# Low halves of weight groups moved three projection pieces behind the high halves, and the W products moved in front of the search's update

## The chip, the cores and the metric

The kernel runs on one core of one Trainium2 chip. The metric is device time in microseconds (us) for one execution, the median of several runs.

## The reference, cut to what matters

One decoder layer over 1024 tokens of width 1024. One input projection feeds three head groups: a gated DeltaNet (4 heads of 128, short causal convolution on q, k and v, chunked delta rule), a sparse attention whose keys are picked by a small indexer (top 256 of up to 1024 keys a token), and a cross-attention into 256 memory tokens.

```python
h = x @ w_in[l]                                   # all projections of the layer
qkv = silu(_short_conv(concat([q_a, k_a, v_a]), conv_w[l]))
# DeltaNet, per head and chunk:
sol = triangular_solve(m, concat([v * beta, k_beta * exp(g)]))   # u, w
def step(state, inp):
    v_new = u_i - w_i @ state
    o = qg @ state + a_i @ v_new
    state = state * gl + kd.T @ v_new
# sparse attention, per token:
score = sum_j(relu(q_idx_j @ k_idx) * w_idx_j)    # then the 256 largest
_, idx = lax.top_k(score, topk)
...
y = concatenate([o_a, o_s, o_m]) @ w_out[l]
x = _layernorm(DEEPNORM_ALPHA * x + y, ln_g[l], ln_b[l])
```

## The kernel before

`make_plan` writes one list of steps; every engine walks it in order and executes what belongs to it, waiting on semaphores. So the place of a step in the list sets its place in the queue of each engine that has part in it. `woven` mixes three things: the steps of the DeltaNet solve and scan of one head, the projection work of the next head (`todo`), and the search for the 256th largest score. A bare number in `steps` is a stretch; in it the plan places a due `update`, then projection units, then one `count` group.

**Projections.** The weights come in 32 groups of 128 columns; 30 of them are split. Products are made in three matmuls of 512 columns: high by high, high by low, low by high (L862 to L864). A *piece* is two of eight chunks of one half of the tokens, that is 6 matmuls; a group has 8 pieces. A group is split by `("split", name)`: ScalarE copies the raw weights to the high half (in the trace `ring_split<-ring`, L1598), VectorE subtracts to get the low half (L1254, `ring_split<-ring,ring_split`, both inputs in SBUF). `with_splits` puts the split of a group where the group before it begins. TensorE waits for the low half before a group's first piece.

**Search.** 32 rounds find the threshold bit by bit. In each, ScalarE counts with six activations (`count`, L1681, widths 1024, 384, 896, 512, 768, 640), and VectorE makes the next candidate in six small operations (`update`, L1307 to L1324) that wait for the six counts; the first count of the next round waits for L1323.

**Solve and scan of head h.** Block inverses are refined by levels (`M`, `XY`). Then `GB` and `KB` prepare the keys of head h+1: VectorE scales the two halves of the keys (L1422 and L1423, each twice; their other input is in PSUM), GpSimd multiplies SBUF by SBUF (L1856 and L1861, each twice, 128x512). `nw` makes the W products of head h (L1043 on TensorE, two copies L1598 `arena<-bank` on ScalarE), needed from the second scan step. `scanV` b (L1051, L1057; copy to `vnew` by VectorE, L1458) and `scanS` b (L1068, L1072, L1073; new state `dn_s` by VectorE, L1466 or L1468; output added by VectorE, L1227 or L1230) alternate over b = 0 to 7. The values' convolution taps (L1216 to L1220) stand between them. Four PSUM banks of pool "D" go round, so the output product of step 0 takes the bank that the first `nw` copy frees.

The order of `("nw", h)` stands in these lines of the plan:

```python
                steps += [*keys_scaled(after)[0], 1.5, *keys_scaled(after)[1], 1.5]
            else:
                steps += [1.5, 1.5]
...
        steps += [*pair("nw", h), 1]
```

## Time and profile before

| | before |
|---|---|
| median of 3 runs | 856.08 us (855.95 to 856.45) |
| profiled execution, device time | 857.43 us |
| its span | 855.6 us |
| mean granted TensorE clock | 0.961 |
| TensorE busy | 764.7 us (89%) |
| VectorE busy | 492.4 us (58%) |
| ScalarE busy | 461.6 us (54%) |
| GpSimd busy | 145.9 us (17%) |

The span is from the first to the last instruction; the device time lies 1.83 us above it. Busy shares are averages over stages: start and index scores to about 160 us, the four DeltaNet heads to about 576 us, attention and output after that. A row of the trace gives the start, the duration, the engine and the line, and in brackets how long the engine had been idle before it and what ended the idle time.

### The profile page before, as it was taken

How to read it: one execution, taken by the hardware profiler on the slowest of the kernel's cores; microseconds unless marked ns; L12 is line 12 of the kernel's file. 1: busy time of each engine (PE TensorE's matmuls, PEld its weight loads, DVE VectorE, ACT ScalarE, POOL GpSimd, SP SyncE). 2: the span in 40 equal slices, each digit the busy share in tenths (PEclk: the TensorE clock that was granted, in tenths of full speed). 3: DMA queues.
4: the chain of work that ended last, by engine and by line, in shares of the span. 5: the costliest groups of instructions: out<-in, count | busy, mean ns of one | idle time of the engine just before them, and what ended most of it. 6: DMA issues, size and time to landing. Idle time of an engine off the chain costs nothing.

```text
span 855.6 us, 11422 instructions
## 1 busy us (share of the span) xinstructions
PE 764.7 (89%) x3996; PEld 621.1 (73%) x3996; DVE 492.4 (58%) x1068; ACT 461.6 (54%) x1045; POOL 145.9 (17%) x248
## 2 busy tenths in 40 slices
PE   6999969899997899789998899885798998998975
PEld 5888858688886789678886788663466776774764
DVE  5633868846655475554654477853556456636532
ACT  5423566789768875888768742224543333332310
POOL 0000000063011510142111420001003033302330
PEclk9999979999999999999998999997889999999998
DMA  9312110125002320023001231009201122121201
GB/s 358 101 50 75 49 38 26 37 66 140 27 26 65 86 82 25 26 77 105 25 26 62 59 124 50 25 33 311 99 1 62 39 72 87 55 60 46 74 25 49
DMA packets 56424, 60.87 MB, mean 71 GB/s; under 512 B 16048, under 2 KB 42928, under 8 KB 55984
## 3 DMA queue, kind: packets, MB, share of 16 engines
q1 hardware_dynamic: 56368, 60.15, 21.4%
q8 instruction: 32, 0.52, 0.2%
q14 instruction: 24, 0.20, 0.1%
HBM read 45.46 MB, written 14.68 MB: 70 GB/s over the span
## 4 chain that ended last, share of the span: by engine, by line
PE 62%; DVE 16%; ACT 13%; issue 6%; DMA 2%; SPq 1%; POOL 0%; DVEq 0%; ACTq 0%; POOLq 0%
PE bank L854 16%; PE bank L862 9%; PE bank L864 9%; PE bank L863 9%; PE bank L868 3%; ACT cst L1681 3%; PE bank L1098 2%; PE bank L1126 2%; PE bank L1018 2%; PE bank L1033 2%; PE bank L1031 2%; PE bank L1005 1%; DVE score L1301 1%; ACT ring_split L1598 1%; DVE mix_lo L1548 1%
## 5 line engine op out<-in xcount | busy, mean ns | idle before, releaser
L862 PE MATMUL bank<-x_hi,ring_split 128*128 128x512 f32 x480 | 200.4, 417 | 7.6 <-DVE x_lo L1246 7.2
L864 PE MATMUL bank<-x_hi,ring_split 128*128 128x512 f32 x480 | 190.9, 398 | 0.0
L863 PE MATMUL bank<-x_lo,ring_split 128*128 128x512 f32 x480 | 190.7, 397 | 0.0
L1681 ACT ACTIVATE cst<-score,sel 128x1024 bf16<-128x1024 f32 (+2 forms) x192 | 166.9, 874 | 24.7 <-DVE sel L1323 24.7
L862 PEld LDWEIGHTS bank<-x_hi,ring_split 128*128 128x128 f32 x480 | 92.6, 193 | 23.4 <-DVE ring_split L1254 7.9
L864 PEld LDWEIGHTS bank<-x_hi,ring_split 128*128 128x128 f32 x480 | 92.1, 192 | 20.6
L863 PEld LDWEIGHTS bank<-x_lo,ring_split 128*128 128x128 f32 x480 | 92.7, 193 | 15.3
L1598 ACT ACTIVATE arena<-bank 128x512 f32<-128x512 f32 (+1 forms) x108 | 49.7, 499 | 35.0 <-PE bank L868 10.5
L1782 ACT ACTIVATE arena<-arena,misc 128x512 f32<-128x512 f32 (+7 forms) x32 | 24.8, 775 | 80.5 <-DVE misc L1518 80.5
L1254 DVE TENSOR_TENSOR ring_split<-ring,ring_split 128x1024 fp32r<-128x1024 f32 x30 | 38.8, 1295 | 43.0 <-ACT ring_split L1598 42.9
L854 PE MATMUL bank<-w_out_hi,mix_hi 128*128 128x512 f32 x128 | 56.0, 437 | 6.7 <-DVE mix_lo L1548 4.2
L1568 DVE SCALAR_TENSOR_TENSOR arena<-qkvT,bank 128x512 f32<-128x512 f32 x16 | 11.0, 688 | 81.2 <-PE bank L854 81.2
L1856 POOL TENSOR_TENSOR arena<-arena,hsc 128x512 f32<-128x512 f32 x8 | 8.3, 1040 | 276.4 <-ACT arena L1738 276.4
L868 PEld LDWEIGHTS bank<-cst,arena 128*128 128x128 f32 x320 | 39.3, 148 | 19.1 <-issue 9.3
L1301 DVE SCALAR_TENSOR_TENSOR score<-arena,wis,score 128x384 f32<-128x384 f32 (+3 forms) x70 | 46.0, 658 | 11.8 <-ACT arena L1669 5.8
L854 PE MATMUL bank<-w_out_lo,mix_hi 128*128 128x512 f32 x128 | 52.6, 411 | 0.0
L1669 ACT ACTIVATE arena<-bank 128x384 f32<-128x384 f32 (+3 forms) x80 | 38.8, 524 | 25.2 <-DVE score L1301 19.7
L1843 POOL TENSOR_TENSOR arena<-arena,cst 128x512 f32<-128x512 f32 x24 | 32.5, 1377 | 115.2 <-DVE arena L1207 51.5
L868 PE MATMUL bank<-cst,arena 128*128 128x128 f32 x320 | 47.3, 284 | 5.0 <-DVE arena L1423 3.7
L854 PE MATMUL bank<-w_out_hi,mix_lo 128*128 128x512 f32 x128 | 51.5, 403 | 0.0
L1098 PE MATMUL bank<-cT,arena 128*128 128x512 f32 (+5 forms) x96 | 40.5, 534 | 12.2 <-DVE misc L1512 10.3
L1098 PEld LDWEIGHTS bank<-cT,arena 128*128 128x128 f32 x96 | 17.8, 199 | 32.0 <-DVE misc L1512 18.1
(246 smaller groups left out, 1442.3 us busy)
## 6 DMA issues: line engine op xcount, KB each, us to landing
ring<-in_w_groups SPq DMA_DIRECT2D x30, 512.0 KB, 3.5
x_raw<-in_x_t SPq DMA_DIRECT2D x8, 512.0 KB, 9.1
side_z<-stage SPq DMA_DIRECT2D x16, 256.0 KB, 2.1
w_out_sb<-in_wout_t SPq DMA_DIRECT2D x2, 2048.0 KB, 13.0
zgT<-side_z SPq DMA_DIRECT2D x8, 512.0 KB, 3.9
qkvT<-in_x SPq DMA_DIRECT2D x8, 512.0 KB, 4.7
out_y<-arena SPq DMA_DIRECT2D x8, 512.0 KB, 2.8
ring<-in_wmem_t SPq DMA_DIRECT2D x2, 1024.0 KB, 4.7
```

The costliest lines, as they stand in the source:

```text
L854: last = nc.tensor.matmul(dst, w, r, start=(i == 0), stop=(i == len(pairs) - 1))
L862: nc.tensor.matmul(dst, hi, xh, start=(c == 0), stop=False)
L863: nc.tensor.matmul(dst, hi, xl, start=False, stop=False)
L864: last = nc.tensor.matmul(dst, lo, xh, start=False, stop=(c == KT - 1))
L868: return nc.tensor.transpose(dst, src, ident[0:n, 0:n])
L1098: nc.tensor.matmul(ps(e)[:, 0:hi - lo], qab[:, h * P:(h + 1) * P], cT[:, lo:hi], start=True, stop=True).then_inc(fill_of(e), 1)
L1254: v.tensor_tensor(lo, whole, hi.bitcast(F32), ALU.subtract).then_inc(weights_split, 1)
L1301: last = v.scalar_tensor_tensor(score[:, at + lo:at + hi], r[:, 0:hi - lo], w, score[:, at + lo:at + hi], ALU.mult, ALU.add)
L1598: return sc.activation(dst, src, ACT.Copy, scale=scale)
L1669: sc.activation(rbuf[(order[e] - 1) % 3][:, 0:hi - lo], ps(e)[:, 0:hi - lo], ACT.Relu, scale=IXD ** -0.5).then_inc(release_of(e), 1)
L1681: sc.activation(signs[order[e] % 2][:, 0:w], score[:, score_at(b):score_at(b + 1)], ACT.Sign, scale=-1.0, bias=candidate[:, b - 2:b - 1], ...
L1843: g.tensor_tensor(quad(row(a, R_UO[s % 2])), quad(row(a, R_U)), rep(cst[:, C_LEV + s * P:C_LEV + (s + 1) * P], 4), ALU.mult).then_inc(leve ...
```

## The change

Two edits. `with_splits` gives the low half a plan step of its own, `("low", name)`, which VectorE executes; the high half keeps the step `("split", name)` on ScalarE. Where the group before consists of projection or side pieces, the low half stands in front of its fourth piece instead of its first. Splits that the plan writes out by hand (the first groups, `out0` to `out7`) keep both halves together. And `nw` moves from behind the last stretch of the solve to the front of it.

```diff
+LOW_BEHIND = 4
...
             if s == NLEV - 1 and more:
-                steps += [*keys_scaled(after)[0], 1.5, *keys_scaled(after)[1], 1.5]
+                steps += [*keys_scaled(after)[0], 1.5, *keys_scaled(after)[1], *pair("nw", h), 1.5]
+            elif s == NLEV - 1:
+                steps += [1.5, *pair("nw", h), 1.5]
             else:
                 steps += [1.5, 1.5]
...
-        steps += [*pair("nw", h), 1]
+        steps += [1]
...
-    steps, seen, done = [], set(), {e[1] for e in plan if e[0] == "split"}
+    steps, seen, used, late = [], set(), 0, []
+    done = {e[1] for e in plan if e[0] == "split"}
     for e in plan:
         g = group_of(e)
-        if g and g not in seen:
-            seen.add(g)
-            for ahead in groups[len(seen):len(seen) + 1]:
-                if ahead not in done and ahead not in ("mk", "mv"):
-                    steps.append(("split", ahead))
-                    done.add(ahead)
+        if g:
+            used += 1
+            if g not in seen:
+                seen.add(g)
+                used = 1
+                for ahead in groups[len(seen):len(seen) + 1]:
+                    if ahead not in done and ahead not in ("mk", "mv"):
+                        steps.append(("split", ahead))
+                        done.add(ahead)
+                        late = [("low", ahead)]
+                        if e[0] not in ("proj", "side"):
+                            steps += late
+                            late = []
+            if used == LOW_BEHIND:
+                steps += late
+                late = []
         steps.append(e)
+        if e[0] == "split":
+            steps.append(("low", e[1]))
...
-                elif k == "split":
+                elif k == "low":
                     name = e[1]
-                    dve.wait_ge(weights_hi_ready, order[e])
+                    dve.wait_ge(weights_hi_ready, order["split", e[1]])
```

The changed file is 16 lines longer at these places, so L1254 of before is L1270 after, and so on.

ScalarE's queue at the end of the solve of head 1. Before (L1598 `x2` are the copies of the W products, L1681 the counts):

```order
L1598 ACTIVATE hbuf<-bank 128x512
L1681 ACTIVATE cst,sel<-score,sel 128x768
L1681 ACTIVATE cst,sel<-score,sel 128x640
L1681 ACTIVATE cst,sel<-score,sel 128x1024
L1681 ACTIVATE cst,sel<-score,sel 128x384
L1598 ACTIVATE arena<-bank 128x512 x2
L1681 ACTIVATE cst,sel<-score,sel 128x896
```

And of the change:

```order
L1614 ACTIVATE hbuf<-bank 128x512
L1697 ACTIVATE cst,sel<-score,sel 128x768
L1697 ACTIVATE cst,sel<-score,sel 128x640
L1614 ACTIVATE arena<-bank 128x512 x2
L1697 ACTIVATE cst,sel<-score,sel 128x1024
L1697 ACTIVATE cst,sel<-score,sel 128x384
L1697 ACTIVATE cst,sel<-score,sel 128x896
```

The two copies have moved in front of the first two counts of the next round. On TensorE the W products moved ahead by one piece.

VectorE's queue at the same place, from the last level of the solve to the first scan step. Before (the last row here is followed by L1216 and L1466):

```order
L1254 TENSOR_TENSOR ring_split<-ring,ring_split 128x1024
L1453 TENSOR_TENSOR arena<-arena,bank 128x4x64 x2
L1440 TENSOR_TENSOR arena<-bank,cst 128x512 x2
L1418 TENSOR_TENSOR hsc<-hsc,sc 128x8
L1419 TENSOR_TENSOR hsc<-hsc,sc 128x8
L1422 TENSOR_TENSOR arena<-bank,hsc 128x512
L1423 TENSOR_TENSOR arena<-bank,hsc 128x512
L1422 TENSOR_TENSOR arena<-bank,hsc 128x512
L1423 TENSOR_TENSOR arena<-bank,hsc 128x512
L1307 TENSOR_TENSOR sel<-sel 128x6
...
L1458 COPY vnew<-bank 128x128
L1254 TENSOR_TENSOR ring_split<-ring,ring_split 128x1024
```

And of the change:

```order
L1469 TENSOR_TENSOR arena<-arena,bank 128x4x64 x2
L1456 TENSOR_TENSOR arena<-bank,cst 128x512 x2
L1434 TENSOR_TENSOR hsc<-hsc,sc 128x8
L1435 TENSOR_TENSOR hsc<-hsc,sc 128x8
L1438 TENSOR_TENSOR arena<-bank,hsc 128x512
L1439 TENSOR_TENSOR arena<-bank,hsc 128x512
L1270 TENSOR_TENSOR ring_split<-ring,ring_split 128x1024
L1438 TENSOR_TENSOR arena<-bank,hsc 128x512
L1439 TENSOR_TENSOR arena<-bank,hsc 128x512
L1323 TENSOR_TENSOR sel<-sel 128x6
...
L1474 COPY vnew<-bank 128x128
L1232 TENSOR_SCALAR qkvT<-hbuf,cw 128x512
```

One low half has moved from the front of the solve's last subtraction to between the two halves of the keys' scaling; the next one has left the place behind the first `vnew` copy.

VectorE's queue in the middle of the scan of head 1, before:

```order
L1324 TENSOR_TENSOR sel<-sel 128x6
L1254 TENSOR_TENSOR ring_split<-ring,ring_split 128x1024
L1468 SCALAR_TENSOR_TENSOR dn_s<-dn_s,sc,bank 128x128
L1230 TENSOR_TENSOR oall<-oall,bank 128x128
L1458 COPY vnew<-bank 128x128
```

And of the change:

```order
L1340 TENSOR_TENSOR sel<-sel 128x6
L1484 SCALAR_TENSOR_TENSOR dn_s<-dn_s,sc,bank 128x128
L1246 TENSOR_TENSOR oall<-oall,bank 128x128
L1474 COPY vnew<-bank 128x128
L1484 SCALAR_TENSOR_TENSOR dn_s<-dn_s,sc,bank 128x128
L1246 TENSOR_TENSOR oall<-oall,bank 128x128
L1270 TENSOR_TENSOR ring_split<-ring,ring_split 128x1024
```

The low half that stood between the update and the new state has moved behind two scan steps.

## Rows read from the trace of the kernel before

**Rows 1.** The page: busy time of the engines, and the low halves' group.

```profile
PE 764.7 (89%) x3996; PEld 621.1 (73%) x3996; DVE 492.4 (58%) x1068; ACT 461.6 (54%) x1045; POOL 145.9 (17%) x248
L1254 DVE TENSOR_TENSOR ring_split<-ring,ring_split 128x1024 fp32r<-128x1024 f32 x30 | 38.8, 1295 | 43.0 <-ACT ring_split L1598 42.9
```

**Rows 2.** What TensorE waited for, 160 to 540 us: total, times, longest.

```profile
PE bank L1051 <- DVE oall L1230: 8.7, 5, 3.2
PE bank L1057 <- DVE dn_s L1466: 8.2, 3, 2.7
PE bank L1073 <- ACT arena L1598: 4.4, 3, 1.5
PE bank L868 <- DVE arena L1423: 3.7, 2, 3.2
```

**Rows 3.** Timeline, TensorE: head 1's W products, and its waits in the scan.

```profile
347.04 1.95 PE L1043 MATMUL bank<-arena 128*128 128x128 f32 x16
...
355.19 0.49 PE L1073 MATMUL bank<-vnew,arena 128*128 128x128 f32 x2 [1.46 <-ACT arena L1598]
360.90 0.46 PE L1057 MATMUL bank<-dn_s,arena 128*128 128x128 f32 x2 [2.73 <-DVE dn_s L1466]
362.94 0.49 PE L1068 MATMUL bank<-vnew,arena 128*128 128x128 f32 x2 [0.18 <-DVE vnew L1458]
381.62 0.49 PE L1051 MATMUL bank<-arena 128*128 128x128 f32 x2 [2.65 <-DVE oall L1230]
```

**Rows 4.** Timeline, ScalarE, from the end of the solve into the scan of head 1.

```profile
352.82 1.15 ACT L1681 ACTIVATE cst<-score,sel 128x1024 bf16<-128x1024 f32 x1 [1.65 <-DVE sel L1323]
...
354.56 1.06 ACT L1598 ACTIVATE arena<-bank 128x512 f32<-128x512 f32 x2
355.52 1.03 ACT L1681 ACTIVATE cst<-score,sel 128x896 bf16<-128x896 f32 x1
...
379.67 0.35 ACT L1598 ACTIVATE oall<-bank,sc 128x128 f32<-128x128 f32 x1
```

**Rows 5.** Timeline, VectorE, the same stretch of head 1.

```profile
348.25 0.68 DVE L1422 TENSOR_TENSOR arena<-bank,hsc 128x512 f32<-128x512 f32 x1
...
351.20 0.71 DVE L1307 TENSOR_TENSOR sel<-sel 128x6 f32<-128x6 f32 x1 [1.67 <-ACT cst L1681]
...
358.81 1.23 DVE L1254 TENSOR_TENSOR ring_split<-ring,ring_split 128x1024 fp32r<-128x1024 f32 x1 [5.62 <-ACT ring_split L1598]
...
362.59 0.29 DVE L1458 COPY vnew<-bank 128x128 f32<-128x128 f32 x1
```

**Rows 6.** Timeline, VectorE, in front of the third wait of head 1.

```profile
379.87 1.24 DVE L1254 TENSOR_TENSOR ring_split<-ring,ring_split 128x1024 fp32r<-128x1024 f32 x1 [0.56 <-ACT ring_split L1598]
...
381.29 0.28 DVE L1230 TENSOR_TENSOR oall<-oall,bank 128x128 f32<-128x128 f32 x1
```

**Rows 7.** Timeline, GpSimd, during the keys' scaling: first and last of four.

```profile
347.86 1.04 POOL L1856 TENSOR_TENSOR arena<-arena,hsc 128x512 f32<-128x512 f32 x1 [35.67 <-ACT arena L1738]
...
350.85 1.04 POOL L1861 TENSOR_TENSOR arena<-arena,sc 128x512 f32<-128x512 f32 x1
```

**Rows 8.** Timeline: a low half beside two GpSimd operations of that kind.

```profile
197.16 2.54 POOL L1843 TENSOR_TENSOR arena<-arena,cst 128x512 f32<-128x512 f32 x2
197.62 3.16 DVE L1254 TENSOR_TENSOR ring_split<-ring,ring_split 128x1024 fp32r<-128x1024 f32 x1 [2.76 <-ACT ring_split L1598]
```

**Rows 9.** Windows, TensorE: busy, instructions, granted clock, DMA, GB/s.

```profile
255.00:260.00 5.00, 3.54 (x17) 1.00 0.30 105
380.00:385.00 5.00, 3.38 (x15) 0.79 0.01 3
400.00:440.00 40.00, 40.00 (x252) 1.00 0.12 39
455.00:460.00 5.00, 2.27 (x13) 0.80 0.01 2
460.00:465.00 5.00, 5.00 (x16) 0.52 0.00 0
```

## Prediction

> **What bounds the kernel now.** I read the page first: TensorE is busy for 764.7 of 855.6 us, no other engine for more than 492.4 [rows 1]. So a change pays only where TensorE stands still. The same page makes the low halves look like a good prey: VectorE sat idle for 42.9 us in front of 30 of them, waiting for ScalarE's high halves [rows 1]. But VectorE is not the bound, and idle time there is worth only what TensorE loses by it. I therefore asked for TensorE's waits in the stretch of the heads, 160 to 540 us [rows 2]: four waits make up 25.0 us (8.7 + 8.2 + 4.4 + 3.7). Three of them come once in each of heads 0, 1 and 2. The change touches all three, and the timeline of head 1 shows them [rows 3]:
>
> - First, at 355.19, 1.46 us, for a copy of the W products: these stand behind two counts of a new search round [rows 4].
> - Second, at 360.90, 2.73 us, for the first new state: it stands behind the low half at 358.81, for which VectorE idled 5.62 us [rows 5].
> - Third, at 381.62, 2.65 us, for an output addition at 381.29, behind the low half at 379.87 [rows 6].
>
> The sum over three heads is near 20 us. Whoever stops here predicts 836. The next question is what ends last when the wait is gone, and for that I read the queues of ScalarE and VectorE beside TensorE.
>
> **What is late next at the first two waits.** VectorE walks its queue in order: new state, update, one tap, `vnew` of step 1. TensorE's step S1 needs that `vnew`; before, it came at 362.59 and TensorE took it at 362.94 [rows 5, 3]. The update waits for six counts, so `vnew` of step 1 hangs on ScalarE's counts and not on the low half. With the first two waits gone TensorE reaches S1 some 4 us (1.46 + 2.73) earlier and stands there. What S1 gains is what the round of counts gains, and no more. This is the step on which I disagree with the 20 us.
>
> **Term 1, the W copies.** ScalarE idles 1.65 us before the count at 352.82, since the update, which waits for the six counts, only starts at 351.20 [rows 4, 5]. The two copies cost 0.96 us of its queue (354.56 to 355.52) [rows 4]. TensorE makes the products at 347.04 to 348.99 [rows 3] and after the change one piece sooner, so they are there when ScalarE comes to the copies at 351.2. The copies fit in the gap (0.96 < 1.65): the counts behind them, and the next update, come 0.96 us earlier. The piece that the products overtake is not the last of its half group, so no copy waits for it. Term 1: -0.96 us a head.
>
> **Term 2, the low half between the keys.** Its new place is 348.25, between the two halves of the scaling, and GpSimd starts four back-to-back operations with SBUF inputs at 347.86, ending at 351.89 (350.85 + 1.04) [rows 5, 7]. If nothing contended, it would cost nothing: VectorE idles 1.67 us before the update [rows 5], and the low half takes 1.24 us [rows 6]. But one low half in the trace took 3.16 us instead of 1.23: it started 0.46 us behind a pair of GpSimd operations and ended at 200.78, 1.08 us after their end at 199.70 [rows 8]. And the update's first operation took 0.71 us at 351.20 and ended at 351.91, 0.02 us after GpSimd's last [rows 5, 7]. So operations of the two engines that read two SBUF operands shut each other out, and the update is already held by GpSimd's run. A low half put inside that run either waits for it or makes it longer. I take the middle case: the low half waits for the two operations that were issued before it (to 349.86), GpSimd's last two wait for the low half, the run ends 1.2 us later, at 353.1, and the update's first operation with it. Nothing: 0. Middle: +1.2. Upper end: the low half waits for three operations (to 350.9), runs to 352.0, the second pair of scalings takes 1.2 us, and the update waits for the fourth operation until 353.8: +1.9. I take +1.2, as the row with 3.16 us shows that a low half does wait for more than the running operation.
>
> The Trainium skill ("SBUF — State Buffer", section "SBUF: two separate sides") says that a VectorE operation with two SBUF inputs and a GpSimd operation that reads SBUF take one shared port pair, and that whoever starts first holds it for a whole instruction. By that rule alone the low half would wait only to the end of the operation under way, 0.6 us; the trace agrees that there is a lock, but its row with 3.16 us shows a wait over two operations. In the sum both readings give the longer GpSimd run, so the term stays.
>
> Terms 1 and 2 together: +0.2 us at S1, against -0.96 without contention.
>
> **Term 3, the third wait.** Between S1 and this place the trace shows ScalarE and the updates in close step, so they carry the +0.2 on. Before, the low half ran from 379.87, the output addition ended at 381.57 and TensorE went on at 381.62 [rows 3, 6]. After, the low half stands two scan steps later. The addition needs ScalarE's scaled output, which ends at 380.02 (379.67 + 0.35) [rows 4]; so it ends at about 380.35 and TensorE goes on at 380.4: -1.2 us, less the +0.2 carried: -1.0. Here nothing takes the place of the wait: the low half in its new place has 2 us of idle VectorE time ahead of the next `vnew`, and TensorE is busy without a break from 400 to 440 [rows 9], so what is gained stays. Heads 0 and 2 show the same pattern.
>
> **Edits costed at nothing.** The prologue's wait of 3.2 us (most of the 3.7 [rows 2]) loses a low half in front of the scalings, some 0.45 us on VectorE by my estimate from the rows of the low half, but TensorE's next product waits for ScalarE's copies behind the counts, whose order is the same. In head 3 VectorE has no idle time to give: its selection steps fill it, and the low half only changes its place among them. W products in head 3: no counts are left there. The other low halves stand where TensorE was fully busy; each new place is some microseconds ahead of the group's first piece (about 5 pieces), the tightest near 203, with 0.3 us.
>
> **Sum.** Per head -0.96 + 1.2 - 1.2 = -1.0; three heads: -3.0 us. The profiled execution took 857.43 us, 1.35 above the median of 856.08; the gain is a difference, so it is taken from the median: 853.1 us.
>
> **The clock, left out of the sum.** After idle spells the granted clock fell: 0.80 and 0.52 behind head 2's first two waits, 0.79 behind head 1's third; behind head 0's, with the same waits, it stayed at 1.00 [rows 9]. 0.52 over 5 us is 2.4 us of matmul time, 0.80 and 0.79 are 1.0 us each. After the change the idle time at the first two waits is one spell of over 4 us at S1, and that at the third is shorter. The one may bring more drops, the other fewer. A drop behind S1 is partly hidden by what is left of the third wait (about 1.3 us). I take zero, with up to 2 us a side.
>
> **Rivals.**
> A, no contention (0.2): the low half slips into VectorE's idle time. S1 comes 0.96 earlier, the third place 2.2 (0.96 + 1.2): -6.6 us, 849.5; with shorter spells and one or two drops fewer down to 847. For it: in rows beside the one of 3.16 us, other low halves took 1.2 to 1.35 us. Against: none of them lay beside a GpSimd run.
> B, the gain is eaten (0.2): term 2 is at its upper end, +1.9; S1 comes 0.9 us later, and the third place gains 1.2 - 0.9 = 0.3. Three heads: -0.9 us, 855.2, no change that can be told. For it: the low half of 3.16 us let two operations pass.
> C, slower (0.1): the gathered spell at S1 halves the clock in all three heads. The place is the first 5 us behind S1; the price is the 2.4 + 1.0 us that head 2's rows show, less 1.3 us hidden, so 2.1 in each of the three heads, 6.3, against the 3.0 gained: +3.3, 859.4. It decides from 1.0 us a head. Against it: head 0 bore 4.2 us of waits at full clock.
> My forecast has 0.5.
>
> **Numbers.** A change below 0.2%, 1.7 us, can hardly be told from none with this kernel. Faster is below 854.4: rival A (0.2) and most of my own case (0.44 of 0.5), and a little of B: 0.66. Same is 854.4 to 857.8: the rest of B, a part of mine, some of C: 0.25. Slower: 0.09. Range: from 848.5 (most of A) to 856.8 (B with a drop); my own case alone is 851 to 855.
>
> **What the profile after should show.** The `nw` copies (L1614) directly behind the count of 640, in ScalarE's gap; no TensorE wait for `arena` at L1089, none for `dn_s` at L1073, and in their place a wait of 3.5 to 5 us at L1084 for `vnew` (L1474), in three heads. The low half (L1270) between the scalings (L1438, L1439) with 2 us or more, or GpSimd's L1872 and L1877 with longer spans; the update's L1323 ending about 1.2 us later relative to the last count. The third wait at L1067 at about half. I am wrong if that low half costs nothing, if S1's wait is not there because counts come earlier than I think, if TensorE waits at L878 for a low half, or if the granted clock changes by more than a hundredth of its mean.

## The result, and the profile after

The changed kernel takes 852.01 us (median of 13 executions, 849.47 to 854.31); the kernel before took 856.45 us beside it (13 executions, 854.52 to 860.81). The ratio is 0.9944, with a 95% interval from 0.9929 to 0.9958: 0.56% faster. Forecast were 853.1 us and a range from 848.5 to 856.8. The profiled execution took 854.07 us with a span of 852.3 us, 3.3 us under the span before; the rest of this document shows that these 3.3 us are the small remainder of larger gains and losses. This execution is one of the three slowest of the thirteen, and its mean granted clock of TensorE, 0.959, is the lowest among them (the highest is 0.966). So what follows of time lost to the clock is told of such an execution, and a middle one may have lost less.

The page of the changed kernel, busy times and the group of the low halves (they answer to [rows 1]; the names of lines have moved by 16, L1254 is L1270 now):

```profile
PE 765.4 (90%) x3996; PEld 622.0 (73%) x3996; DVE 495.9 (58%) x1068; ACT 461.4 (54%) x1045; POOL 152.3 (18%) x248
L1270 DVE TENSOR_TENSOR ring_split<-ring,ring_split 128x1024 fp32r<-128x1024 f32 x30 | 38.3, 1276 | 7.4 <-ACT ring_split L1614 7.1
```

VectorE's idle time in front of the low halves went from 42.9 to 7.1 us. That is 36 us of idle time gone on an engine that doesn't set the end, for 3.3 us of the span. GpSimd is busy for 6.4 us more with the same 248 instructions, so its operations were held up.

What TensorE waited for from 160 to 540 us (total, times, longest), the answer to [rows 2]:

```profile
PE bank L1084 <- DVE vnew L1474: 13.4, 6, 3.8
PE bank L884 <- DVE arena L1439: 3.2, 2, 2.7
PE bank L1067 <- DVE oall L1246: 3.0, 5, 1.3
```

Two of the four old waits are gone (for the W copies and for the first new state), one has shrunk from 8.7 to 3.0 us, one is hardly changed (3.7 to 3.2), and a wait for `vnew` that hardly existed before (0.4 us) has taken 13.4 us. Head 1 in TensorE's timeline, the answer to [rows 3]:

```profile
356.08 0.49 PE L1084 MATMUL bank<-vnew,arena 128*128 128x128 f32 x2 [0.67 <-DVE vnew L1474]
364.70 0.49 PE L1084 MATMUL bank<-vnew,arena 128*128 128x128 f32 x2 [3.80 <-DVE vnew L1474]
382.54 0.49 PE L1067 MATMUL bank<-arena 128*128 128x128 f32 x2 [0.46 <-DVE oall L1246]
```

These three starts are the key to all that follows. I call the start of the product with `vnew` in scan step n "Sn" (S0 at 356.08 and S1 at 364.70 here; at 353.24 and 362.94 before) and compare the times from one to the next. In the windows of the changed kernel (us; then busy time of TensorE, its weight loads, VectorE, ScalarE and GpSimd; then the granted clock, DMA share and GB/s) TensorE's clock falls behind S1 in each of heads 0 to 2, and no longer behind the third wait, where it was 0.79 before [rows 9]:

```profile
265.00:270.00 5.00, 2.02 (x8) 1.92 (x9) 3.78 (x12) 3.81 (x10) 0.00 (x0) 0.70 0.00 0
270.00:275.00 5.00, 5.00 (x25) 4.52 (x24) 2.74 (x5) 3.79 (x11) 0.29 (x1) 0.61 0.15 56
360.00:365.00 5.00, 1.20 (x6) 0.68 (x5) 2.37 (x9) 4.19 (x10) 0.00 (x0) 1.00 0.00 0
365.00:370.00 5.00, 5.00 (x26) 4.54 (x25) 3.13 (x6) 4.97 (x13) 0.00 (x0) 0.66 0.00 0
380.00:385.00 5.00, 4.54 (x28) 3.66 (x27) 2.12 (x10) 5.00 (x12) 3.90 (x15) 1.00 0.40 135
460.00:465.00 5.00, 5.00 (x17) 4.42 (x18) 2.90 (x5) 4.98 (x12) 0.00 (x0) 0.50 0.00 0
```

Worked out from TensorE's timeline, summed over heads 0 to 2 (us; "end" is S0 of head 3). The kernels of the experiments below stand in the same table, so that each can be read against the two:

| kernel | S0 of head 0 | S0 to S1 | S1 to S2 | S2 to S4 | S4 to S5 (third wait) | S5 to S6 | S6 to next S0 | end |
|---|---|---|---|---|---|---|---|---|
| before | 256.9 | 30.2 | 18.6 | 23.6 | 22.4 | 13.2 | 179.0 | 543.9 |
| changed | 259.4 | 25.9 | 24.0 | 23.4 | 13.1 | 11.7 | 182.1 | 539.5 |
| W products alone (e1) | 257.5 | 28.9 | 17.6 | 23.4 | 20.4 | 11.7 | 179.2 | 538.6 |
| low halves alone (e2) | 259.6 | 28.7 | 17.3 | 23.9 | 14.4 | 11.7 | 183.0 | 538.5 |
| update late (e5) | 259.9 | 14.0 | 34.1 | 23.3 | 20.8 | 12.9 | 181.8 | 546.8 |
| k1 and keys (e8) | 257.8 | 25.9 | 22.9 | 23.4 | 13.7 | 11.7 | 180.3 | 535.5 |
| scan's low halves (e11) | 257.6 | 25.9 | 24.9 | 23.4 | 13.0 | 11.7 | 180.9 | 537.3 |
| third wait's alone (e10) | 257.5 | 27.8 | 17.8 | 23.6 | 14.2 | 11.7 | 181.3 | 533.9 |

Changed against before: 2.4 us lost up to the first S0, 4.3 gained up to S1, 5.4 lost behind S1, 0.2 gained from S2 to S4, 9.2 at the third wait and 1.6 at the step behind it, 3.1 lost between the heads. The sum is 4.5 us of gain at the end of head 2; the tail from there to the end of the span gives 1.2 of it back, which leaves the 3.3.

Idle time and clock can be told apart, since TensorE does the same matmuls in each of these stretches (some 68 records in a head from S0 to S2; one or two can be missing from a trace). From S0 to S2, over the three heads, it stood idle for 12.9 us before and 11.4 after, and was busy for 35.9 us before and 38.5 after: 1.5 us gained by waiting less, 2.6 lost to the lower clock. From S4 to S6 it was idle for 8.2 us before and 0.8 after, and busy for 27.4 and 24.0: 7.4 us gained by waiting less, 3.4 by the clock that no longer falls there.

### The profile page after: what moved, and what is told of

Same layout as the page of the kernel before. It is cut to its first block, busy times and chain, and to the rows that moved or that the text cites. A ratio compares the mean times of both kernels' runs of the same rounds, so it can differ in the third digit from the quotient of the medians.

```text
span 852.3 us, 11425 instructions
## 1 busy us (share of the span) xinstructions
PE 765.4 (90%) x3996; PEld 622.0 (73%) x3996; DVE 495.9 (58%) x1068; ACT 461.4 (54%) x1045; POOL 152.3 (18%) x248
## 4 chain that ended last, share of the span: by engine, by line
PE 58%; DVE 17%; ACT 14%; issue 8%; DMA 2%; SPq 1%; POOL 0%; DVEq 0%; ACTq 0%; POOLq 0%
PE bank L870 16%; PE bank L878 8%; PE bank L880 8%; PE bank L879 8%; ACT cst L1697 5%; PE bank L884 3%; PE bank L1114 2%; PE bank L1142 2%; PE bank L1034 2%; PE bank L1049 2%; PE bank L1021 2%; PE bank L1047 2%; ACT ring_split L1614 2%; DVE score L1317 1%; DVE mix_lo L1564 1%
## 5 line engine op out<-in xcount | busy, mean ns | idle before, releaser
L1114 PE MATMUL bank<-cT,arena 128*128 128x512 f32 (+5 forms) x96 | 40.8, 537 | 12.2 <-DVE misc L1528 10.4
L1270 DVE TENSOR_TENSOR ring_split<-ring,ring_split 128x1024 fp32r<-128x1024 f32 x30 | 38.3, 1276 | 7.4 <-ACT ring_split L1614 7.1
```

The source lines that it names most:

```text
L1114: nc.tensor.matmul(ps(e)[:, 0:hi - lo], qab[:, h * P:(h + 1) * P], cT[:, lo:hi], start=True, stop=True).then_inc(fill_of(e), 1)
L1270: v.tensor_tensor(lo, whole, hi.bitcast(F32), ALU.subtract).then_inc(weights_split, 1)
```

## The experiments

They ran in three groups, each beside the kernel before on the same chip: e1 to e4 (before at 857.85 us), e5 to e8 (856.41), e9 to e11 and the changed kernel once more (856.43). The intervals of the ratios are some 0.2 to 0.3% wide to each side, so medians that differ by 1 to 2 us are told apart by their traces, not by their times. And a trace is one execution: that of e1 is the fastest of its twelve and that of e5 the slowest, which matters where their rows in the table are compared.

**e1, the W products alone.** `with_splits` and the low halves as before; the moved `pair("nw", h)` kept:

```
     for e in plan:
         g = group_of(e)
-        if g:
-            used += 1
...
+        if g and g not in seen:
+            seen.add(g)
```

> The W products alone, low halves as before. My theory (S1's wait is set by the round of counts, and the two copies go into ScalarE's gap): the first wait of 1.46 us goes, the search runs 0.96 us earlier from there, so S1 comes 1 us earlier in each of three heads; the low half in front of the first new state stays, and so does the third wait: 2 to 3 us faster than before, 853.5 to 854.5. Rival (the gain of the change is all from the low halves, and the copies only change places with the counts): within 1 us of before.

Measured: 857.19 us (852.18 to 861.09), ratio 0.9995 (0.9971 to 1.002). No change: the rival holds, the theory's 853.5 to 854.5 does not. The profiled execution took 852.18 us, so its rows serve for the order of events and not for its length. TensorE's waits (160 to 540 us), and from its timeline the second one in head 1:

```profile
PE bank L1059 <- DVE dn_s L1468: 10.5, 3, 3.5
PE bank L1053 <- DVE oall L1232: 8.5, 5, 3.2
```

```profile
360.71 0.77 PE L1059 MATMUL bank<-dn_s,arena 128*128 128x128 f32 x2 [3.50 <-DVE dn_s L1468]
```

The wait for the W copies is gone, and the one behind it has grown from 2.73 to 3.50 us. VectorE's timeline says why:

```profile
358.62 1.22 DVE L1256 TENSOR_TENSOR ring_split<-ring,ring_split 128x1024 fp32r<-128x1024 f32 x1 [4.66 <-ACT ring_split L1600]
...
360.28 0.29 DVE L1468 COPY dn_s<-bank 128x128 f32<-128x128 f32 x1
360.49 0.15 DVE L1309 TENSOR_TENSOR sel<-sel 128x6 f32<-128x6 f32 x1
...
362.41 0.29 DVE L1460 COPY vnew<-bank 128x128 f32<-128x128 f32 x1
```

The state still stands behind the low half, which waits for its high half in ScalarE's queue. But term 1 is there: the update begins 6.48 us behind S0 (7.43 before) and `vnew` of step 1 stands 8.40 us behind S0 (9.35 before), so both come 0.95 us earlier. TensorE did not collect it, because its clock fell behind the wait of 3.50 us:

```profile
361.71 0.63 PE L865 MATMUL bank<-x_lo,ring_split 128*128 128x512 f32 x1
363.77 0.38 PE L1070 MATMUL bank<-vnew,arena 128*128 128x128 f32 x2
```

The same matmul takes 0.39 us at full clock. From the product with the new state (360.71) to S1 (363.77) it needed 3.06 us, against 2.04 us before, and S1 came when `vnew` had been ready for 1.1 us. So S0 to S1 takes 9.41, 9.76 and 9.72 us in the three heads, against 9.70, 9.70 and 10.79.

**e2, the low halves alone.** The W products where they were:

```
-                steps += [*keys_scaled(after)[0], 1.5, *keys_scaled(after)[1], *pair("nw", h), 1.5]
-            elif s == NLEV - 1:
-                steps += [1.5, *pair("nw", h), 1.5]
+                steps += [*keys_scaled(after)[0], 1.5, *keys_scaled(after)[1], 1.5]
...
-        steps += [1]
+        steps += [*pair("nw", h), 1]
```

> The low halves alone, W products as before. My theory: third wait shorter by 1.2 us a head and the clock's fall behind it gone, against 0.8 us a head for the low half among GpSimd's operations and 1.5 us for the low half of k1 in front of a stage copy at 202 to 204 us: between 2 us faster and 1 us slower than before. In its trace the first wait (for a copy of the W products) is there with 1.5 to 2.5 us in three heads, and the head's last scan steps have no wait over 1.4 us. Rival (the low halves carry the whole gain of 4.4 us): 852.

Measured: 852.65 us (850.26 to 853.36), ratio 0.9941 (0.9918 to 0.9964). The whole gain of the change, within what can be told, is there without the W products: the rival holds. Its waits:

```profile
PE bank L1082 <- DVE vnew L1472: 6.2, 6, 1.4
PE bank L1065 <- DVE oall L1244: 4.8, 5, 1.3
PE bank L1087 <- ACT arena L1612: 4.4, 3, 1.5
```

The third wait is cut here as in the changed kernel (S4 to S5 is 14.4 us over three heads, against 22.4 before). What I had in mind, that the W products give 1 us a head of time and the low halves give and take about the same, is refuted by e1 and e2 together. The clock fell here too, at another place: 0.82 from S0 to S1 in each of the three heads, behind the wait of 1.46 us, which follows one of 0.67 us for the first `vnew` by half a microsecond of work. Before, the same 1.46 us without the 0.67 in front brought no fall.

**e3, the low half in front of both scaled keys.** In heads 1 to 3 `("low", side)` goes from behind `("KB", h, 0)` to ahead of it:

```
+    for h in range(1, DNH):
+        at, end = plan.index(("KB", h, 0)), plan.index(("KB", h, 1))
+        low = next(e for e in plan[at:end] if e[0] == "low")
+        plan.remove(low)
+        plan.insert(at, low)
```

> The changed kernel with one low half of each of heads 0 to 2 moved from between the two halves of the keys' scaling to in front of them, into VectorE's idle time before the inverse norms and ahead of GpSimd's run. Contention theory: the low half takes 1.23 us instead of 1.73, GpSimd's second operation 1.04 instead of 2.02, and the next round of counts starts 0.8 us earlier after the end of the last; 1.5 to 2.5 us faster than the change, about 850. Rival (VectorE's queue has room there, the lock costs nothing on the path): same time as the change within 0.5 us.

Measured: 851.95 us (850.02 to 852.7), ratio 0.9931 (0.9905 to 0.9957). By its time this is the changed kernel, as the rival had it, and the gain of 1.5 to 2.5 us can't be seen; the trace shows the contention taken away. In head 0 of the changed kernel, VectorE's and GpSimd's timelines:

```profile
253.60 1.73 DVE L1270 TENSOR_TENSOR ring_split<-ring,ring_split 128x1024 fp32r<-128x1024 f32 x1
256.55 0.69 DVE L1323 TENSOR_TENSOR sel<-sel 128x6 f32<-128x6 f32 x1
257.28 0.97 DVE L1334 TENSOR_TENSOR sel<-sel 128x6 f32<-128x6 f32 x1
```

```profile
253.20 1.04 POOL L1872 TENSOR_TENSOR arena<-arena,hsc 128x512 f32<-128x512 f32 x1 [35.47 <-ACT arena L1754]
254.20 2.02 POOL L1877 TENSOR_TENSOR arena<-arena,sc 128x512 f32<-128x512 f32 x1
256.19 1.04 POOL L1872 TENSOR_TENSOR arena<-arena,hsc 128x512 f32<-128x512 f32 x1
257.18 1.04 POOL L1877 TENSOR_TENSOR arena<-arena,sc 128x512 f32<-128x512 f32 x1
```

and in e3:

```profile
250.07 1.21 DVE L1280 TENSOR_TENSOR ring_split<-ring,ring_split 128x1024 fp32r<-128x1024 f32 x1
257.37 0.72 DVE L1333 TENSOR_TENSOR sel<-sel 128x6 f32<-128x6 f32 x1 [1.67 <-ACT cst L1707]
258.12 0.17 DVE L1344 TENSOR_TENSOR sel<-sel 128x6 f32<-128x6 f32 x1
```

In the changed kernel the low half waits some 0.5 us for the GpSimd operation under way, GpSimd's second operation then takes 2.02 instead of 1.04 us, and of the update two small operations are held (0.69 and 0.97 instead of 0.17). In e3 the low half takes 1.21 us and only one small operation is held, as before the change. The span from the last count to the next round's first falls back from 2.43 us to the 1.65 us of before: contention cost 0.8 us a head, and the S0-to-S0 times of e3 are shorter by 1.6 and 0.8 us behind heads 0 and 1 and the same behind head 2. The wait of 0.67 us for `vnew` at S0 is gone too.

**e4 and e7, the prologue's low half of k1.** In the changed kernel the M products near 211 came 1.5 us later than before. In e4 `("low", "k1")` and `("update", 3)` change places:

```
+    at = plan.index(("low", "k1"))
+    plan[at - 1:at + 1] = plan[at], plan[at - 1]
```

In e7 the low half goes directly behind its high half, as before the change:

```
+    plan.remove(("low", "k1"))
+    plan.insert(plan.index(("split", "k1")) + 1, ("low", "k1"))
```

> The changed kernel with the low half of group k1 alone put back in front of the update of round 3, so that it no longer stands between that update and the copy of a result to the staging buffer. Theory: the copy (L1298-like, near 203.6 in the change) is 1.2 us earlier, SyncE's store and the block inverses' transfers behind it too, and TensorE's waits at 204 and 213 us go: 1.2 to 1.6 us faster than the change. Rival (these 1.6 us are made up later by TensorE's waits in the scan): same time within 0.3 us.

> The changed kernel with the low half of the one group k1 put back directly behind its high half; all other groups as changed. In the changed kernel this low half stands between update 3 and the copy of the stage tile at 203, and the copy, SP's stores behind it and the M products at 213 are 1.4 to 1.55 us later than before. Theory: that delay is the low half's own 1.2 us on VectorE and is carried to the end, so the M products go back to 211.5 and the time falls by about 1.5 us, to 850.5. Rival: the 1.5 us are taken up by the waits of the scan (the update's wait behind the first scan product is 3.8 us and ends with ScalarE's counts), and the time stays within 0.5 us of 852. Wanted rows: the copy of stage near 202.3 instead of 203.6, the first M product near 211.6.

Measured: e4 851.78 us (849.66 to 854.0), ratio 0.9933 (0.9909 to 0.9956); e7 850.51 us (849.84 to 851.11), ratio 0.9927 (0.9906 to 0.9948). In the changed kernel the low half stands in front of the copy of `stage` in VectorE's timeline, and with it SyncE's queue, shown below it, comes later:

```profile
202.48 1.23 DVE L1270 TENSOR_TENSOR ring_split<-ring,ring_split 128x1024 fp32r<-128x1024 f32 x1
203.62 0.68 DVE L1298 COPY stage<-bank 128x512 f32<-128x512 f32 x1
```

```profile
204.75 0.63 SPq L802 DMA_DIRECT2D diag_x<-arena  x1
```

Before, the copy of `stage` stood at 202.23 and the first store of `diag_x` at 203.37. The first M product (sixteen matmuls with one start) came at 211.51 before, and in the changed kernel, e4 and e7 at:

```profile
213.06 2.02 PE L1034 MATMUL bank<-arena 128*128 128x128 f32 x16 [0.66 <-issue]
```

```profile
212.40 2.02 PE L1042 MATMUL bank<-arena 128*128 128x128 f32 x16 [0.35 <-issue]
```

```profile
212.23 2.02 PE L1041 MATMUL bank<-arena 128*128 128x128 f32 x16 [0.25 <-issue]
```

Part of these differences is a shift of the whole trace that lies further ahead. From TensorE's block of sixteen near 201 to the first M product it took 10.37 us before, 11.69 in the changed kernel, 11.05 in e4 and 10.77 in e7. So the stretch lost 1.3 us, of which e4 gives back 0.6 and e7 0.9, and my expectation for e7 (211.6) was 0.6 us off, though its time came out as expected; the time of e4 is that of its rival. The rest is a second contention, as e9 shows below: before, GpSimd's scaling behind the triangular solve began at 197.16 [rows 8]; in the changed kernel it began at 198.72 and in e7 at 199.66, since the solve met a low half on its way (side0's at 186.87 to 188.09 in the changed kernel, where GpSimd's 64x48 step took 1.18 us against 0.59). In e7 its last copy waits for the low half, and the scaling ends behind the update's start and holds it. VectorE and then GpSimd in e7:

```profile
197.93 1.27 DVE L1277 TENSOR_TENSOR ring_split<-ring,ring_split 128x1024 fp32r<-128x1024 f32 x1 [2.87 <-ACT ring_split L1621]
201.40 0.80 DVE L1330 TENSOR_TENSOR sel<-sel 128x6 f32<-128x6 f32 x1 [2.19 <-ACT cst L1704]
```

```profile
198.19 1.50 POOL L1914 COPY arena<-arena 64x256 f32<-64x256 f32 x1
199.66 2.52 POOL L1866 TENSOR_TENSOR arena<-arena,cst 128x512 f32<-128x512 f32 x2
```

**e5, the update behind `vnew`.** Each update that lay between two scan steps goes behind the next step's `vnew`:

```
+    for h in range(DNH):
+        for b in range(1, NB):
+            v = plan.index(("scanV", h, b))
+            held = [e for e in plan[plan.index(("scanS", h, b - 1)):v] if e[0] == "update"]
+            for e in held:
+                plan.remove(e)
+                plan.insert(plan.index(("scanV", h, b)) + 1, e)
```

> The changed kernel with each update of the search that stood between two scan steps moved behind the copy of vnew of the next scan step, in all heads. Theory: the 3.8 us in which TensorE waits at the second scan step of heads 0 to 2 is vnew queued on VectorE behind an update that waits for ScalarE's counts; with the update behind it the wait goes to under 1 us, and since ScalarE then gets its next update only a little later, what returns at the later steps is less: 3 to 8 us faster than the changed kernel, 844 to 849. Rival: ScalarE's counts bound these stretches, the update comes later and so the next counts, and the wait comes back whole in the third wait and in the taps: within 1 us of 852, or slower by 1 to 3 us through the later counts.

Measured: 856.91 us (852.0 to 860.82), ratio 1.0007 (0.9986 to 1.0029): 5 us slower than the changed kernel, all of its gain gone, and more than the rival allowed. The profiled execution took 860.82 us, the slowest of the twelve. The first half of the theory holds: S0 to S1 takes 4.65 us a head, down from 8.62. The rest fails. TensorE's waits:

```profile
PE bank L1033 <- ACT arena L1626: 9.6, 4, 3.0
PE bank L1079 <- DVE oall L1258: 8.3, 6, 2.3
```

The next product needs a copy that stands behind counts in ScalarE's queue, so S1 to S2 takes 34.1 us over three heads instead of 24.0. And the third wait is back: there ScalarE idles for an update that now comes too late,

```profile
377.19 1.15 ACT L1709 ACTIVATE cst<-score,sel 128x1024 bf16<-128x1024 f32 x1 [2.52 <-DVE sel L1351]
```

which the theory had put at little. The waits of the two kernels fit one reading, that ScalarE's queue of counts limits the first two steps of the scan, whichever wait shows it.

**e8, k1 and the keys together.** The edits of e7 and e3:

```
+    plan.remove(("low", "k1"))
+    plan.insert(plan.index(("split", "k1")) + 1, ("low", "k1"))
+    for h in range(1, DNH):
...
+        plan.insert(at, low)
```

> The changed kernel with two placements changed: the low half of group k1 directly behind its high half, and the low halves of the three side groups in front of both scaled keys (there GpSimd does not run yet) instead of between them. Theory: the two gains add: 1.5 us of the prologue and, from the run with the keys alone (S0 to S0 periods 95.1 and 94.5 against 96.7 and 95.3, low half 1.21 us against 1.73), 1 to 2 us more: 849 to 850.5. Rival: what the keys gain is lost in the waits behind, and the time is that of the run with k1 alone, within 0.5 us.

Measured: 849.41 us (847.2 to 851.97), ratio 0.9914 (0.9888 to 0.994). The theory's range holds. By time alone it can't be told from e7, whose six executions lie between its own; in the traces "end" is 4.0 us ahead of the changed kernel and 2.2 us ahead of e7.

**e6, three edits.** The low half in front of the keys (e3), k1 as in e4, the late update (e5):

```
+        plan.insert(at, low)
...
+    plan[at - 1:at + 1] = plan[at], plan[at - 1]
...
+                plan.insert(plan.index(("scanV", h, b)) + 1, e)
```

> Three edits at once on the changed kernel: the low halves of the side groups in front of both scaled keys, the low half of k1 in front of update 3 (and so before the stage copy, too, but hidden in the wait for the counts), and the updates behind vnew. Theory: if the late update pays by itself, this is the sum: 3 to 8 us for it and 1 to 2 for the others: 842 to 848. Rival: the late update brings nothing or costs, and this lies within 1 us of that run, near 851.

Measured: 854.49 us (849.79 to 856.06), ratio 0.9968 (0.9951 to 0.9985). Slower than the changed kernel, and outside both ranges. The late update spoils it as it spoils e5; the two other edits give 2.4 us against e5.

**e9, the whole prologue as before, and the keys.** As e8, and `side0` and `side1` behind their high halves again:

```
+    for g in ('side0', 'side1', 'k1'):
+        plan.remove(("low", g))
+        plan.insert(plan.index(("split", g)) + 1, ("low", g))
```

> The changed kernel with the low halves of the prologue's three groups (side0, side1, k1) directly behind their high halves again, and those at the scaled keys in front of both keys. Against the run with k1 and keys alone only side0 and side1 differ. Theory: the low half of side0 lies in the changed kernel at 186.87 to 188.09, where GpSimd runs the small steps of the triangular solve, and GpSimd's steps took longer there (the 64x48 step 1.18 us against 0.59): the chain that ended at 197.2 before ends at 198.8. With side0 back at 181, where GpSimd waits, GpSimd's 128x512 step starts near 197.2 again, and the first M product is at 211.5 instead of 212.2: 0.7 us faster than with k1 and keys alone, near 848.7. Rival: the solve is not what the M products wait for, and the time stays at 849.4 within 0.3 us, the M product at 212.2.

Measured: 848.22 us (846.54 to 850.77), ratio 0.9898 (0.9867 to 0.9929). The solve did go faster. GpSimd's last copy of it and the scaling in e9, and TensorE's first M product:

```profile
197.69 0.63 POOL L1920 COPY arena<-arena 64x256 f32<-64x256 f32 x1
198.29 2.56 POOL L1872 TENSOR_TENSOR arena<-arena,cst 128x512 f32<-128x512 f32 x2
```

```profile
212.35 1.95 PE L1047 MATMUL bank<-arena 128*128 128x128 f32 x16
```

In e8 the scaling begins at 199.73, and the M product, at 212.23, has an idle time of 0.17 us in front of it. Here it has none, and stands 10.37 us behind the block of sixteen near 201, as before the change, against 10.80 in e8. So the mechanism holds, and 0.4 us, not 0.7, were all that was left to gain. That the M product is no earlier than in e8 comes from further ahead: the block of sixteen near 177 stands at 176.98, against 176.41 in e8 and 176.11 before. The traces of e1, e10 and e11, whose prologue is that of the kernel before, are 0.6 us later than before there as well, so shifts of this size say nothing. The times of e8 and e9 can't be told apart.

**e11, only the scan's low halves late.** The prologue's, the q and v groups' and those at the keys are behind their high halves again; late are side3, side5, side7, k2, k3 and side8:

```
+    for g in ("side0", "side1", "k1", "side2", "side4", "side6", "side9", "side10", "side11", "q1", "q2", "q3", "v1", "v2", "v3"):
+        plan.remove(("low", g))
+        plan.insert(plan.index(("split", g)) + 1, ("low", g))
```

> As the run named third alone, and the low halves of side3, side5 and side7 (the groups that begin at the first scan step) late too; so all late low halves are those that lie in a scan, and the prologue, the q and v groups and the groups at the scaled keys are as before. Theory: this keeps both gains (the second scan step 1.1 us shorter, as in the changed kernel, the third wait gone) and sheds the two costs (low half between the keys 0.8 us a head, prologue 1.5 us): the changed kernel less 3 to 4 us, 847.5 to 849.5. Rival: counts on ScalarE set the scan's pace, so that what comes earlier waits there: within 1 us of 850.

Measured: 849.13 us (848.23 to 850.95), ratio 0.9914 (0.9887 to 0.9941), as the theory had it, but also within the rival's range (849 to 851), so the time doesn't decide between them. In the trace the costs are gone, but S1 to S2 takes 24.9 us, more than in the changed kernel.

**e10, only those of the third wait late.** The same loop with side3, side5 and side7 in it; late are k2, k3 and side8 alone:

```
-    for g in ("side0", "side1", "k1", "side2", "side4", "side6", "side9", "side10", "side11", "q1", "q2", "q3", "v1", "v2", "v3"):
+    for g in ("side0", "side1", "k1", "side2", "side3", "side4", "side5", "side6", "side7", "side9", "side10", "side11", "q1", "q2", "q3", "v1", "v2", "v3"):
```

> Of the changed kernel only this is kept: the W products in front of the update, and the low halves of the three groups that begin in the middle of a scan (k2, k3 and side8) made three pieces behind. All other low halves stand again directly behind their high halves, as before the change. Theory: the whole gain comes from the third wait of heads 0 to 2, whose step took 7.3 to 7.6 us before and 4.0 to 4.6 after; the other late low halves bring nothing and cost 0.8 us at each pair of scaled keys and 1.5 us in the prologue. Then S4 to S5 is at most 5 us in each head, the step behind the keys is as in the kernel with the W products alone, and the time is 3 to 6 us under before: 850.5 to 853.5. Rival: the gain needs the late low half near the second scan step too (side3, side5, side7), since the kernel with the W products alone waited 3.5 us there against 2.73 before: then it lies within 1.5 us of before, 855 to 858.

Measured: 847.37 us (846.69 to 849.35), ratio 0.9892 (0.9863 to 0.9922), the fastest kernel of the study, and 3 us under what the theory allowed. S4 to S5 is 4.33, 4.65 and 5.18 us in the three heads, where the theory said at most 5. From e1 this kernel differs only in the three low halves, and e1 was no faster than before. The three without the W products were not run, so what the two share between them is not shown. **The changed kernel once more**, beside it:

> The changed kernel itself once more, to have it beside the others on the same chip. Both theories expect 852 us, 0.5% under before, and it sets what the three others are measured against; if it lies more than 1 us from 852.0, differences of that size between calls say nothing.

851.13 us (849.67 to 853.12), ratio 0.9936 (0.9911 to 0.9962). All six executions of e10 lie below all seven of the changed kernel. Three low halves moved do more than twenty-one. Why e10's trace is ahead of e11's is seen behind S0 of head 1. TensorE's timeline of e11, its windows, and the same two views of e10, with two rows of its head 2 at the end:

```profile
361.89 0.80 PE L1092 MATMUL bank<-vnew,arena 128*128 128x128 f32 x2 [3.82 <-DVE vnew L1482]
```

```profile
360.00:365.00 5.00, 3.10 (x10) 2.77 (x11) 4.54 (x11) 4.31 (x9) 0.00 (x0) 0.53 0.00 0
365.00:370.00 5.00, 5.00 (x29) 4.54 (x28) 2.29 (x5) 4.37 (x11) 1.65 (x2) 0.79 0.27 89
```

```profile
358.68 0.46 PE L1081 MATMUL bank<-dn_s,arena 128*128 128x128 f32 x2 [3.50 <-DVE dn_s L1490]
```

```profile
355.00:360.00 5.00, 1.50 (x7) 1.14 (x6) 3.21 (x10) 4.07 (x11) 0.00 (x0) 0.92 0.02 5
360.00:365.00 5.00, 5.00 (x25) 4.43 (x24) 2.49 (x6) 4.98 (x14) 0.00 (x0) 0.73 0.00 0
```

```profile
453.17 0.46 PE L1081 MATMUL bank<-dn_s,arena 128*128 128x128 f32 x2 [3.50 <-DVE dn_s L1490]
455.20 0.49 PE L1092 MATMUL bank<-vnew,arena 128*128 128x128 f32 x2 [0.18 <-DVE vnew L1482]
```

With the second wait left in place TensorE stands for 3.50 us instead of 3.82, and it loses less to the clock behind it. From S0 to S2 of the three heads TensorE was busy for 39.3 us in e11 and 34.9 in e10, with the same matmuls, and idle for 11.4 and 10.7. So of the 5.2 us between them (50.7 against 45.6 us) the clock made 4.4 and the waiting 0.8; e11 gets 1.2 us back at the third wait. In head 2 of e10 the clock stayed at 1.00, and S0 to S1 took 8.74 us, 0.96 less than the 9.70 of before: that is term 1 of the prediction to the hundredth, with no low half moved at this place. The trace is again one execution: three of the six of e10 have a mean clock of 0.958, like all six of e11 (0.958 to 0.959), and took 847.37 to 849.35 us, so the clock explains the two traces better than the two medians. What makes the clock fall in one head and not in another is not settled: no run changed the idle spell alone.

## Why the prediction was right in the time, and where its steps failed

The time was 1.1 us from the forecast by luck: large errors of both signs cancelled, the gain at the third wait against the clock behind S1 and the costs put at nothing. By its own steps:

- **"S1 hangs on the counts and not on the low half"** held where both parts are made: the waits for the W copies and for the first state are gone, and TensorE stands 3.80 us at L1084 in three heads, within the 3.5 to 5 us named. This is why 20 us of waits were not 20 us of gain. e5 confirms it from the other side: take the update from the queue, and the next ScalarE copy is late.
- **Term 1, -0.96 us.** This held. S0 to S1 fell by 1.08 us in heads 0 and 1, and the W products alone make 0.95 of it: `vnew` of step 1 stands 9.35 us behind S0 before, 8.40 in e1 and 8.27 in the changed kernel. That e1 is no faster is due to the clock, which the prediction had left out: behind a wait of 3.50 us it fell in all three heads of e1's trace, and where it did not (head 2 of e10) the 0.96 us arrived. e1 itself shows how much the clock weighs: its three fastest executions (852.18 to 853.15 us) have a mean granted clock of 0.961 to 0.965, its two slowest (860.06 and 861.09) one of 0.951.
- **Term 2, +1.2 us.** Measured +0.8. The lock is there, but the low half waited for one operation and not for two, and it took 1.73 us and not "2 us or more". That is the reading by the rule in the Trainium skill ("SBUF — State Buffer", section "SBUF: two separate sides"), and the trace agrees with it at this place: 0.5 us of waiting, then 1.0 us for the GpSimd operation behind. It does not fit the 3.16 us of [rows 8], which came back as 3.35 to 3.53 us in e1, e9, e10 and e11. The upper end of this term, +1.9, does not follow from its own steps: if the low half ends at 352.0, GpSimd's last operation of 1.04 us ends near 353.1 and the second pair of scalings near 353.2, not 353.8.
- **Term 3, -1.0 us.** It measured -3.1 us a head (S4 to S5, 9.2 us over three heads), and 0.5 us a head more in the step behind it; of the two, 2.5 us a head are less waiting and 1.1 the clock. This is the term that was mis-sized most, and its step that failed is "the addition needs ScalarE's scaled output, which ends at 380.02". In the changed kernel the addition stands at 382.21, ahead of that step's scaled output at 382.35, and directly behind the update; it uses the output of the step before. So not 1.2 us of low half went, but all from the update's end to the state at 381.03, 1.7 us. To this came the counts, some 0.4 us closer to S4 than before (the update begins 0.72 us behind S4 in head 1, 1.15 before), and the clock fall, which the shorter wait no longer brings (0.92 and 0.77 in these two steps of head 1 before, 1.00 after).
- **"What is gained stays"** failed in part: a wait for the next addition came up in each head (1.35 us at 295.75, 0.38 at 390.99, 0.52 at 487.00), and at S0 of each of heads 0 to 2 `vnew` is 0.67 us late. The latter is the contention: it is gone in e3 and e8. From S6 to the next S0 the heads lost 2.25 and 0.92 us and gained 0.09.
- **The clock, left out.** Rival C's mechanism came true in all three heads: S1 to S2 is 5.4 us longer in sum. It did not decide, since term 3 was three times as large and the falls behind the third wait went. Its price was set too high, though: 3.4 us for head 2 before, where S0 to S2 took 17.85 us against 15.49 in the two other heads, 2.4 more. The two profiled executions of the changed kernel agree, with 8.52, 7.38, 8.13 and 8.53, 7.38, 8.11 us from S1 to S2, but both have a mean clock of 0.959, and most of the others had 0.961 to 0.966. So that the falls belong to the kernel in every execution is not shown. The sign that was set for the clock, a change of its mean by over a hundredth, stayed silent (0.961 and 0.959), because falls went at one place and came at another.
- **Edits costed at nothing.** The prologue cost 1.3 us between the blocks near 201 and 213. I had checked the low half near 203 only against the first piece of its group ("the tightest near 203, with 0.3 us"), and not what is queued behind it on VectorE: the copy of `stage`, and behind that SyncE's queue down to the M products. No cost of the q and v groups shows: S6 to the next S0 takes 180.3 us in e8, where they are late, and 181.3 in e10, where they are not. Head 3 did cost a little: its S0 to S1 takes 4.53 us against 4.17 before, and 4.17 again in e10 and e11, where its low halves stand as before.
- **Rival A** (849.5) said that nothing contends. With the contention at the keys and the low half of k1 cured, e8 comes to 849.41, but by other sizes than the rival's, so the number is a coincidence. Its counter-argument, that no low half before lay beside a run of GpSimd, was not quite so: one took 1.35 us at 479.37 beside steps of the solve. **Rival B** did not come.

The sum in profiled time was -3.0 and is -3.3, with +1.3 in the prologue, -4.3 ahead of S1 and +5.4 behind it, -10.8 at the third wait and behind it and +3.1 between the heads, none of which stood in it with that size.

## What to carry to other kernels

When several waits of one engine are to be removed, ask for each what its queue's next entry waits for, and try each alone: here twenty-one moved operations and the moved products gave a little over half of what three of the moves gave with the same products (5.3 against 9.1 us beside the same runs of before). An operation that is moved on an in-order queue must be checked against all that is queued behind it there, DMA issues of other queues included, and not only against its own consumer. A gain that comes right behind an idle spell can be lost to the clock, as in e1, and this is seen only if busy and idle time are counted apart over the same matmuls. Whether one long spell costs more than the same idle time in pieces is not shown: over the three heads, S0 to S2 kept TensorE busy for 39.3 us with one spell of 3.8 us (e11), for 34.9 and 36.0 with one of 3.5 (e10, e1), and for 37.4 and 35.9 with pieces (e2, before).

## What the runs showed of the hardware

- TensorE's granted clock fell behind a spell of 3.8 us in every head of the traces of the changed kernel and of e11; the lowest window of 5 us in each head showed 0.50 to 0.66, and 0.50 is the lower of the two levels (1.2 of 2.4 GHz) throughout; projection matmuls took 0.63 us there, against 0.39 to 0.40. From S0 to S2 TensorE was busy for 13.0 to 13.2 us in each head of e11, against 10.8 in the head of e10 at full clock. Behind spells of 3.50 us it fell in two heads of three in e10 (11.9 and 12.2 us) and in all three of e1 (11.9 to 12.1), and in all three of e2 (12.5) behind a wait of 1.46 us that follows one of 0.67 us by half a microsecond of work; the same 1.46 us alone brought no fall in the three heads of before.
- A VectorE operation of 128x1024 with two SBUF inputs that meets a run of GpSimd operations waited at the keys for one of them (1.73 us instead of 1.23, and GpSimd's next took 2.02 instead of 1.04), and in the prologue for two (3.16 us before, 3.35 to 3.53 in e1, e9, e10 and e11, each time behind the pair of some 2.5 us). When it starts first, GpSimd's operation waits (1.50 instead of 0.63 us in e7). Which of the first two happens isn't explained by these runs.
